# Two transformer blocks on one core: the second mixing linear on unnormalised slices, the first rotation among the slices, two weight units rounded ahead of a convolution

## The reference, cut to what matters

```
for l in range(2):
    h = rmsnorm(x, attn_norm[l])            # x * rsqrt(mean(x*x) + eps) * gain
    z = h @ w_in[l]                         # split into 18 parts, among them
    #   qI, kI, kB, kD  -> first mixing linear  ("mix1", 512 columns)
    #   fA, wI, vB, vD  -> second mixing linear ("mix2", 204 columns)
    #   qB, qA, kA, vA, qC, ...  -> linears of 512 columns each
    score = sum over h of relu(rope(qI) . rope(kI)) * wI   # picks 128 keys per query
    ... four attention-like branches, gates, w_out ...
    x = x + merged @ w_out[l]
    h = rmsnorm(x, ffn_norm[l])
    u = causal_dwconv(h @ w_up[l], conv_w[l], conv_b[l])   # three taps
    a, b = jnp.split(u, 2, axis=-1)
    x = x + (silu(a) * b) @ w_down[l]
```

## Time and profile before

| | |
|---|---|
| median of three runs | 3088.8 us |
| the profiled execution's own time | 3089.22 us |
| its span, first to last instruction | 3087.3 us |
| busy share PE, PEld, DVE, ACT, POOL | 98%, 79%, 44%, 42%, 45% |
| mean granted TensorE clock | 0.992 |

### The profile page before, as it was taken

One profiled execution on the slowest core, in us unless ns is written; L12 is line 12 of the kernel. 1 busy time (PEld: TensorE's weight loads), 2 busy tenths in 40 slices (PEclk: granted clock), 3 DMA queues, 4 the chain that ended last, 5 costly groups with the idle time before them and its releaser, 6 DMA issues.

```text
span 3087.3 us, 39955 instructions
## 1 busy us (share of the span) xinstructions
PE 3022.4 (98%) x15350; PEld 2442.7 (79%) x15350; DVE 1359.2 (44%) x2174; ACT 1286.5 (42%) x2203; POOL 1385.5 (45%) x1001
## 2 busy tenths in 40 slices
PE   8999999999998999999999999999999999999998
PEld 7778887788887777777888888877777788878887
DVE  7874331411115867563116433167765520263311
ACT  5443343433333445454234443244454533354432
POOL 5335563444444432234454544444322354544543
PEclk9999999999999999999999999999999999999999
DMA  5334242233324322122333333243231233333331
GB/s 156 90 103 145 92 130 79 85 96 98 98 89 97 102 68 76 52 62 86 96 93 96 99 96 96 87 107 100 67 91 38 62 96 98 97 93 96 98 96 65
DMA packets 213690, 283.37 MB, mean 92 GB/s; under 512 B 42522, under 2 KB 122450, under 8 KB 211842
## 3 DMA queue, kind: packets, MB, share of 16 engines
q1 hardware_dynamic: 211026, 275.66, 30.8%
q0 software_dynamic: 864, 2.99, 0.3%
q10 hardware_dynamic: 1616, 2.23, 0.2%
HBM read 265.61 MB, written 4.69 MB: 88 GB/s over the span
## 4 chain that ended last, share of the span: by engine, by line
PE 88%; DVE 7%; ACT 3%; issue 1%; POOL 1%; DMA 0%; ACTq 0%; SPq 0%; DVEq 0%
PE half L707 77%; PE half L1112 2%; PE half L1143 2%; PE half L1129 1%; PE half L1203 1%; POOL wL L2833 1%; DVE arena L2011 1%; PE half L1189 1%; DVE nL L2018 1%; DVE arena L2789 0%; PE half L957 0%; DVE arena L2036 0%; PE half L974 0%; DVE rms L2002 0%; ACT arena L1305 0%
## 5 line engine op out<-in xcount | busy, mean ns | idle before, releaser
L2833 POOL TENSOR_TENSOR wL<-slot,wH 128x512 fp32r<-128x512 f32 (+1 forms) x976 | 1357.1, 1398 | 1660.3 <-ACT wH L1292 1659.3
L1292 ACT ACTIVATE wH<-slot 128x512 fp32r<-128x512 f32 (+1 forms) x976 | 603.3, 625 | 1252.6 <-PE half L707 1247.6
L707 PE MATMUL half<-nH,wH 128*128 128x512 f32 x2336 | 926.5, 397 | 11.3 <-POOL wL L2833 6.4
L707 PE MATMUL half<-nH,wL 128*128 128x512 f32 x2336 | 912.4, 391 | 0.0
L707 PE MATMUL half<-nL,wH 128*128 128x512 f32 x2336 | 911.4, 390 | 0.0
L707 PE MATMUL half<-arena_split,wH 128*128 128x512 f32 (+1 forms) x2432 | 735.3, 385 | 1.8 <-ACT arena L1305 1.4
L707 PEld LDWEIGHTS half<-nH,wH 128*128 128x128 f32 x2336 | 439.4, 188 | 122.6 <-issue 25.3
L707 PEld LDWEIGHTS half<-arena_split,wH 128*128 128x128 f32 x2432 | 451.4, 188 | 94.3 <-issue 3.3
L707 PEld LDWEIGHTS half<-nH,wL 128*128 128x128 f32 x2336 | 439.4, 188 | 93.0
L707 PEld LDWEIGHTS half<-nL,wH 128*128 128x128 f32 x2336 | 439.8, 188 | 89.7 <-issue 1.7
L707 PE MATMUL half<-arena_split,wL 128*128 128x512 f32 (+1 forms) x1216 | 466.5, 384 | 0.0
(11 more groups left out here) (344 smaller groups left out, 2574.3 us busy)
## 6 DMA issues: line engine op xcount, KB each, us to landing
slot<-in_w_in SPq DMA_DIRECT2D x344, 256.0 KB, 2.7
slot<-in_w_up SPq DMA_DIRECT2D x440, 128.0 KB, 2.2
slot<-in_w_down SPq DMA_DIRECT2D x132, 256.0 KB, 2.7
slot<-in_w_branch SPq DMA_DIRECT2D x64, 256.0 KB, 2.6
slot<-in_w_out SPq DMA_DIRECT2D x48, 256.0 KB, 2.8
slot<-in_w_gate SPq DMA_DIRECT2D x88, 128.0 KB, 2.1
arena<-arena SPq DMA_DIRECT2D x40, 256.0 KB, 4.3
slot<-in_w_proj_b SPq DMA_DIRECT2D x16, 256.0 KB, 2.9
```

Of the source, the lines that this page charges most:

```text
L707: mm = pe.matmul(dst, lhsT, rhs, start=(k == 0 and m == 0), stop=(k == last and m == 2))
L1292: act.activation(wH[:, p, 0:cols], slot[:, s, 0:cols], ACT.Copy).then_inc(weights_high, 1)
L2833: pool.tensor_tensor(wL[:, p, 0:cols], slot[:, s, 0:cols], plainly(wH[:, p, 0:cols]), ALU.subtract)\
```

## The change

- `JOBS_LAYER` gets a job `scale` in half 0 between the second mixing linear and qB.
- PE: the first mixing linear has its square sum behind unit 6 instead of 4. The second has no wait for normalised slices any more; behind its unit 5 PE transposes `rms` (the token's 1/root, four times 128x128), so that it stands by token on partitions. qB waits for the normalised slices instead.
- ACT: rounds three units of the second linear ahead of the root, the other five behind it, and qB's units between the slices; copies the transposed scale; reads the second linear in four instructions with the scale, instead of one; the rotation's wait and the copy of the index keys stand behind slice 5, slices 6 and 7 and their weight units behind the first dots' copy.
- DVE: takes the reciprocal, scales the first linear at once, then normalises the slices, with the rotation behind slice 3 (and the product of slice 5).
- ACT, feed-forward part of both layers: `bup2`'s units 0 and 1 are rounded ahead of `conv_last(0)`.
- Some semaphores are merged (`silu_a` and `silu_b`, `zv_stats` and `zv_std`); counts on others are adapted.

```diff
-JOBS_LAYER = ["mix1=0", "ss_at=1", "mix2=1", "qB=0", ...
+JOBS_LAYER = ["mix1=0", "ss_at=1", "mix2=1", "scale=0", "qB=0", ...
@@ PE @@
-                linear("bmix1", stream, l, ready=unnormed("bss_at", l), after=lambda: square_sum("bss_at", l))
-                linear("bmix2", stream, l, tokens=NB, cols=MIX2, ready=normed("bss_at", l))
+                linear("bmix1", stream, l, ready=unnormed("bss_at", l), after=lambda: square_sum("bss_at", l), at=6)
+                def turn_scale():
+                    o = fill("bscale", l)
+                    pe.wait_ge(S["token_rstd"], l + 1)
+                    for b in range(NB):
+                        mm = pe.transpose(o[:, b * P:b * P + P], rms[:, b * P:b * P + P], ident)
+                    mm.then_inc(S["vecs_turned"], 1)
+                linear("bmix2", stream, l, tokens=NB, cols=MIX2, after=turn_scale, at=5)
...
-                        unit(o, name, k, act, l, tokens=tokens, into=...)
+                        unit(o, name, k, act, l, tokens=tokens, ready=normed("bss_at", l) if name == "bqB" else None, into=...)
@@ ACT @@
                     others("bmix1", l)
+                    round_units("bmix2", l, 0, range(3), MIX2)
                     ... root ...
-                second_linear("bss_at", "bmix1", "bmix2", l, cols=MIX2)
-                ahead("bqB", l)
+                round_units("bmix2", l, 0, range(3, KD), MIX2)
+                round_units("bqB", l, 0, [0], 512)
+                round_normed("bss_at", 0, l, "bmix2")
+                round_normed("bss_at", 1, l, "bmix2")
+                act.wait_ge(S["vecs_turned"], 2 * l + 3)
+                h = jobs.half["bscale"]
+                evac(token_rms, ps[h][:, 0:T:P], h)
+                round_units("bqB", l, 0, [1], 512)
+                round_normed("bss_at", 2, l, "bmix2")
+                round_units("bqB", l, 0, [2], 512)
+                round_normed("bss_at", 3, l, "bmix2")
                 done(act, "bmix2", l)
-                evac(mix2, banks(jobs.half["bmix2"], w=MIX2), jobs.half["bmix2"])
-                round_units("bqB", l, 0, [4, 5], 512)
+                read_out(act, "bscale", l)
+                h = jobs.half["bmix2"]
+                for b in range(NB):
+                    ins = act.activation(mix2[:, b, :], ps[h][:, b * T:b * T + MIX2], ACT.Copy, scale=token_rms[:, b:b + 1])
+                ins.then_inc(drained[h], 1)
+                round_units("bqB", l, 0, [3], 512)
+                round_normed("bss_at", 4, l, "bmix2")
+                round_units("bqB", l, 0, [4], 512)
+                round_normed("bss_at", 5, l, "bmix2")
                 act.wait_ge(S["roped"], PRIMED + l * 5 + 1)
                 ... two copies of the index keys ...
+                round_units("bqB", l, 0, [5], 512)
-                round_units("bqB", l, 0, [6, 7], 512)
                 index_relu(1)
+                round_normed("bss_at", 6, l, "bmix2")
+                round_units("bqB", l, 0, [6], 512)
+                round_normed("bss_at", 7, l, "bmix2")
+                round_units("bqB", l, 0, [7], 512)
+                index_relu(2)
                 round_units("bqA", l, 0, [0], 512)
-                index_relu(2)
                 round_units("bqA", l, 0, [1], 512)
                 index_relu(3)
@@ ACT, feed-forward @@
                     elif g:
                         ahead(f"bup{g + 1}" if g + 1 < NG else "bdn0", l)
+                    else:
+                        round_units("bup2", l, 0, [0, 1], 512)
                     conv_last(g)
-                    if g == 0:
-                        round_units("bup2", l, 0, [0, 1], 512)
@@ DVE @@
-            def split_norm(name, gains, l=0, ks=range(KD), between=None):
+            def split_norm(name, gains, l=0, ks=range(KD), between=None, at=1):
...
-                    if between and k == 1:
+                    if between and k == at:
...
-                if l == 0:
-                    dve.wait_ge(S["joined_root"], 1)
-                    link(dve.reciprocal(rms[:, :], rms[:, :]))
-                    split_norm("bss_at", both, l, between=scaled_mix)
-                else:
-                    inverse_root("bss_at", l)
-                    split_norm("bss_at", vec[:, W_AT:W_AT + KD], l, between=scaled_mix)
...
-                rope("bmix1", mix1, 0)
+                if l == 0:
+                    dve.wait_ge(S["token_root"], NB + 1)
+                else:
+                    read_out(dve, "bss_at", l)
+                dve.reciprocal(rms[:, :], rms[:, :]).then_inc(S["token_rstd"], 1)
+                dve.wait_ge(S["token_rstd"], l + 1)
+                scaled_mix()
+                split_norm("bss_at", vec[:, W_AT:W_AT + KD] if l else both, l, between=lambda: rope("bmix1", mix1, 0), at=3)
```

More of the change, by code:

```diff
@@ L137 @@
               "xo0=1", "xo1=0", "up0=1", "ss_ff=0"] + [f"up{g}={1 - g % 2}" for g in range(1, NG)] + ["dn0=0", "vecs=1", "dn1=1"]
-JOBS_LAYER = ["mix1=0", "ss_at=1", "mix2=1", "qB=0", "ix1=1", "ix2=1", "ix3=1", "lf=1", "qA=1", "kA=0", "vA=1",
+JOBS_LAYER = ["mix1=0", "ss_at=1", "mix2=1", "scale=0", "qB=0", "ix1=1", "ix2=1", "ix3=1", "lf=1", "qA=1", "kA=0", "vA=1",
               "ft=0", "fb0=0", "fb1=1", "qC=0", "kC=0", "vC=0", "qD=0", "gC=0", "gt0a=0", "tC=0", "gt1a=0", "gt2a=0",
@@ L1042, in some @@
                             fill(name, l)
-                        unit(o, name, k, act, l, tokens=tokens, into=(lambda j: bank_free(name, j, l)) if name in BY_BANK_B else None)
+                        unit(o, name, k, act, l, tokens=tokens, ready=normed("bss_at", l) if name == "bqB" else None, into=(lambda j: bank_free(name, j, l)) if name in BY_BANK_B else None)
                 def index_dots(b):
@@ L1651, in _ @@
                     done(act, f"aup{g}")
-                    act.activation(sg_a[:, g % 2, :, :], banks(jobs.half[f"aup{g}"], n=2), ACT.Silu).then_inc(S["silu_a"], 1)
+                    act.activation(sg_a[:, g % 2, :, :], banks(jobs.half[f"aup{g}"], n=2), ACT.Silu).then_inc(S["silu"], 1)
                     if g + 1 < NG:
@@ L1699, in _ @@
                     others("bmix1", l)
+                    round_units("bmix2", l, 0, range(3), MIX2)
                     act.wait_ge(S["summed"], nth_norm("bss_at"))
                     h = jobs.half["bss_at"]
-                    act.activation(rms[:, :], ps[h][:, T:2 * T], ACT.Sqrt, bias=eps_square, scale=1.0 / D).then_inc(S["joined_root"], 1)
+                    act.activation(rms[:, :], ps[h][:, T:2 * T], ACT.Sqrt, bias=eps_square, scale=1.0 / D).then_inc(S["token_root"], 1)
                     evac(rms_first, ps[h][:, 0:T], h, ACT.Sqrt, bias=eps, scale=1.0 / D)
@@ L1706, in _ @@
                     others("bmix1", l)
+                    round_units("bmix2", l, 0, range(3), MIX2)
                     root("bss_at", l)
[L1708 to L1712 removed]
+                round_units("bmix2", l, 0, range(3, KD), MIX2)
[9 more added lines that the diff above has]
+                round_normed("bss_at", 3, l, "bmix2")
+                done(act, "bmix2", l)
+                read_out(act, "bscale", l)
[7 more added lines that the diff above has]
+                round_normed("bss_at", 5, l, "bmix2")
                 act.wait_ge(S["roped"], PRIMED + l * 5 + 1)
```

22 lines of the change are left out of this document (11 added, 11 removed).

## The result

The changed kernel takes 3097.15 us (median of 17 runs, 3094.85 to 3099.53) against 3088.51 for the kernel before, run beside it: ratio 1.0032, 95% interval 1.0026 to 1.0039. It is slower by 8.6 us between the medians, 9.9 by the ratio (8.0 to 12.0); 3100 was forecast, and 3080 to 3107 given as the range. The profiled execution has a span of 3095.0 us, 7.7 more than before.

The account below looks back on a forecast made before the run. The prediction took TensorE (PE), busy 98% of the span, to bound the kernel. Its terms, -7.2 - 0.3 + 10.4 + 5.5 + 2.6 = +11.0 us on the profiled 3089.2 (runs' median 0.4 lower), gave 3100, range 3080 to 3107.

Parts of the forecast that it names:

- SL earlier, layer 0: SL is the start of the second mixing linear; in layer 0 it was to come at 971.9 instead of 977.95.
- Part 1: Mixing stage, later square sum and second linear on unnormalised slices: 7.2 us gained in layer 0, 0.3 in layer 1.
- Part 2: Mixing stage, chain from first index dots to forget transposes: 5.2 us later per layer, 10.4 in two.
- scores 2: DVE's second scores in the chain behind the first dots: to meet two subtractions and last to 16.4 us behind the dots.
- copy 2: ScalarE's second copy in the chain behind the first dots: 1.45 us long, ending 10.9 us behind the dots.
- Part 3: Convolution, up weights rounded ahead of it: PE's wait at bup2's unit 2 grows by 2.75 us, twice: 5.5.
- Part 4: Slow clock behind four new PE waits (first dots, bup2's unit 2, both layers): 1.3 us in every second, 2.6.
- The forecast's own range: 2 less or 1.3 more per layer in each of parts 1 and 2, 0 to 6 for clock: 3093 to 3107.
- Rival 1: Mixing stage: slices slip past POOL, end at 12.9, keys copied before PE asks: -10.5 us, 3078; chance 0.15.
- Rival 2: First wait as computed, but the chain from dots to transposes keeps its 13.2 us: +0.6, 3089; chance 0.13.
- Rival 3: Convolution: Part 3 costs nothing and no slow stretch follows there: +4.2 us, 3093; chance 0.12.

Follow-up runs that it names:

- experiment 5: Changed kernel with two of the three instructions of the first rotation left out (part of the computation missing): 3088.75 us, ratio 1.0005 to the kernel before.
- dots_later: Changed kernel, convolution edit undone, rotation behind the fifth slice, forget transposes ahead of the dots, dots behind units 4, 5, 6: 3080.14 us, ratio 0.9981.
- experiments 1 and 2: The two runs conv_undone (1) and conv_only (2): 3087.49 us and 3094.77 us, ratios 1.0005 and 1.0035 to the kernel before.
- conv_only: Kernel before with the convolution edit alone (bup2's units 0 and 1 rounded ahead of group 0's last taps): 3094.77 us, ratio 1.0035.
- rotation_early: Changed kernel with the convolution edit undone and the rotation back behind the second slice: 3093.34 us, ratio 1.0020 to the kernel before.
- keys_first: dots_later with only three of four parts rotated first, the fourth between scores of blocks 2 and 3, forget transposes one unit further ahead: 3076.96 us, ratio 0.9970.
- conv_undone: Changed kernel with the convolution edit undone, everything else of the change kept: 3087.49 us, ratio 1.0005 to the kernel before.
- dots_last: Changed kernel, convolution edit undone, rotation behind the sixth slice, forget transposes ahead of the dots, dots behind units 5, 6, 7: 3087.45 us, ratio 0.9998.
- experiment 3: Kernel before with half of the convolution edit: only bup2's unit 0 rounded ahead of group 0's last taps: 3093.07 us, ratio 1.0021.

## Why the prediction was right

The sum was +11.0 and the time came 8.6 us above the median of before beside it. The three mechanisms were the ones that the traces show; that the sum came so near was in part luck, as the parts tell. By its parts, in us, layer 0 and layer 1:

| step | predicted | the trace |
|---|---|---|
| SL earlier, layer 0 | 6.05 | 5.4 (6.3 less the 0.9 by which this execution already lagged at unit 4 of the first linear) |
| rotation starts, from SL | 16.6 | 17.1, 17.1 |
| rotation's length | 9.4 | 8.0, 8.0 |
| first dots, from SL | 27.5 | 26.45, 26.45 |
| PE's wait there | 4.4 | 4.22, 4.21 |
| waits at third dots, transposes | 2.5, -- | 0.55 and 1.84; 0.72 and 1.84 |
| dots to transposes, more than before | 5.2 | 4.2, 4.4 |
| PE at bup2's unit 2, more than before | 2.75 | 2.76, 2.77 |
| clock, all four waits | 2.6 | 1.6 and 3.1 in the convolution; 0.3 and 0.5 at the dots, in the row of the transposes |

Part 1 was 1 us a layer too dark. GpSimd's subtraction for unit 3 was over before the rotation began (987.65 to 989.16), and the one for unit 4 held up its first instruction by 1.1 us (3.38 us in place of 2.28), so the rotation met one subtraction where I had counted two. The rotation on VectorE, layer 0:

```profile
989.63 3.38 DVE L2556 TENSOR_TENSOR arena<-arena,consts 128x2048 f32<-128x2048 f32 x1
993.05 2.29 DVE L2559 TENSOR_TENSOR arena<-arena,consts 128x2048 f32<-128x2048 f32 x1
995.38 2.29 DVE L2561 TENSOR_TENSOR arena<-arena 128x2048 f32<-128x2048 f32 x1
```

Part 2 held in its mechanism: it is a chain without slack (experiment 5 shows it staying 17 us long when the dots start early, dots_later shows it leaving PE's path when the transposes no longer depend on it). It was 1 us a layer too dear: scores 2 took 4.8 us (1009.63 to 1014.41) and not 5.5, and copy 2 ended 10.6 us behind the dots and not 10.9. So the mixing stage was predicted at +2.9 without clock and is -4.4 + 3.0 = -1.4 by the traces, +1.5 by the run with the edit undone (-1.5 to +4.9).

Part 3 was exact in the wait, and this is where the time went: with the slow stretches 8.9 us by the sum for the edit alone and 8.3 to 9.7 by the run with it undone, the whole loss. Part 4, the clock, was too low and in the wrong place. I spread 2.6 us over four waits, 1.3 of it over the two in the convolution; these cost 1.6 and 3.1 (1.7 and 1.7 in the run with the edit alone), and 3.1 is beyond my bound of 1.6 for one. The two at the dots cost 0.3 and 0.5. Two errors of 3 to 4 us in the profiled execution, the mixing stage too dear and the convolution's clock too cheap, cancelled in the sum. That is luck.

The parts of the traces come to -1.4 + 5.5 + 4.7 = 8.8 us, and with the 0.9 of the lag to 9.7, where the spans differ by 7.7. Some 1.6 of the difference lies in layer 0 behind the mixing stage, where the change has nothing but merged semaphores: in the kernel before the granted clock was 0.94 and 0.98 over two stretches of 20 us from 1080 on, with no wait of PE over 0.3 us in them, and in the changed kernel it was 1.00 there. The forecast's own range, 3093 to 3107, is narrower than its terms: 2 less a layer in each of two parts and no clock give 3089, 1.3 more and 6 of clock give 3109.

Rival 1 needed the slices to slip past GpSimd; 17.1 against its 12.9 refutes it. Rival 2 (the chain behind the dots keeps its length) is refuted by the 4.2 and 4.4. Rival 3 (the convolution edit is hidden) is refuted by experiments 1 and 2.

## What to carry to other kernels

An instruction that waits for a weight's slot to come free takes everything queued behind it along: before moving such a rounding ahead of work on the critical chain, read how long its record waits, not how long it runs. When two engines shut each other out and one feeds the matmul with several things, ask which of them is needed last and what part of it the next consumer reads at all; here three quarters of an instruction first and one quarter in an idle gap gave the fastest of the orders tried. A wait removed ahead of a value that is then late itself (the square sum alone) only changes its name.

## What I had not expected of the hardware

Whether VectorE or GpSimd is in first changes a whole stage of the kernel before. In its profiled execution the rotation began 9.8 us behind SL, and GpSimd's last subtraction of 204 columns was caught behind its first instruction. In the profiled execution of the run with the convolution edit alone, whose mixing stage is the same code, the slowest of the partners' transfers took 6.3 us instead of 5.0, the rotation began 0.9 us later, and the subtraction got in first. GpSimd and PE in the kernel before, layer 0, then GpSimd, VectorE and PE in that run:

```profile
987.80 2.73 POOL L2833 TENSOR_TENSOR wL<-slot,wH 128x204 fp32r<-128x204 f32 x1
...
993.96 0.47 PE L707 MATMUL half<-nH,wH 128*128 128x512 f32 x1 [1.78 <-POOL wL L2833]
```

```profile
987.65 1.44 POOL L2833 TENSOR_TENSOR wL<-slot,wH 128x204 fp32r<-128x204 f32 x2 [1.56 <-ACT wH L1292]
...
989.33 3.15 DVE L2533 TENSOR_TENSOR arena<-arena,consts 128x2048 f32<-128x2048 f32 x1 [0.80 <-DMA arena<-arena]
...
1003.24 1.13 PE L1050 MATMUL half<-arena 64*128 64x256 f32 x8
```

PE's wait of 1.78 at the query projection's start is missing there, and the first dots stand 24.6 us behind SL, where the other layers of that code show 27.8 to 28.9. With a rotation that began 0.9 us later the stage was 4 us shorter. This is one layer of one execution, and no run was made to force the order. It may be part of the scatter of the kernel before (3080.07 to 3092.0 in 17 runs; the changed kernel's 17 lie within 4.7 us); how large a part was not measured.

The other thing is how wait and clock went together. Behind the waits of 3.4 to 5.3 us the granted clock was 0.50 to 0.72 in all ten stretches given here (four above, two behind the dots of dots_later, 0.66 and 0.67 in conv_only, 0.62 and 0.57 behind the 5.25 us of rotation_early). Behind short waits it went either way. It was 1.00 behind 1.7 us (keys_first) and 1.35 us (conv_undone), but 0.65 and 0.64 behind the 1.87 us of dots_last. Behind the three short waits in a row of the kernel before it was 0.66 in layer 0 and 1.00 in layer 1, and behind the 2.4 us of experiment 3 it was 0.65 and 1.00. So the price of a wait of some 2 us changes from layer to layer of one execution, which may be another part of the scatter. The page "TensorE: Matmul & The Clock Gate" of the Trainium skill (Part 1, What's actually happening) has the count of slow matmuls at a kernel's start vary with the phase. Here, behind waits in mid-kernel, it was between 5 and 13 behind six waits of 4.08 or 4.09 us, which agrees.
